# Fetching the down weights of an expert stage from ScalarE's queue, gate and up from SyncE's

## What is computed

```python
def expert_block(args):
    xb, e = args                                   # 128 token rows, an expert
    hid = jax.nn.silu(xb @ w_eg[e]) * (xb @ w_eu[e])    # gate and up, 1024 x 256
    return hid @ w_ed[e]                           # down, 256 x 1024

ys = lax.map(expert_block, (xs, blk_e)).reshape(p_rows, d)
out = jnp.zeros((n, d), h.dtype).at[buf_tok].add(ys * buf_w[:, None])
```

## Time and profile before

| | |
|---|---|
| time, median of 3 runs | 1252.3 us (1246.91 to 1253.53) |
| profiled execution, its own time | 1250.46 us |
| its span, first to last instruction | 1248.4 us |
| TensorE matmul busy | 1108.9 us, 89% |
| VectorE, ScalarE busy | 712.3 us (57%), 564.8 us (45%) |
| hardware DMA queue | 166.65 MB, 38.4% of 16 engines' span |
| software DMA queue | 16.80 MB, 3.6% |

### The profile page before, as it was taken

How to read it: one execution, slowest core, us unless ns; L and a number is a source line. 1 busy time by engine, 2 the same in 40 slices (tenths; PEclk the granted TensorE clock), 3 DMA queues, 4 the chain that set the end, 5 groups by cost and what they waited for, 6 DMA issues and landing times.

```text
span 1248.4 us, 18136 instructions
## 1 busy us (share of the span) xinstructions
PE 1108.9 (89%) x6835; PEld 963.9 (77%) x6835; DVE 712.3 (57%) x832; ACT 564.8 (45%) x756; POOL 327.0 (26%) x276
## 2 busy tenths in 40 slices
PE   3998999999999899999998999329999999999940
PEld 3885888888877788888887888329999999999930
DVE  5874666666055711111114232558888888888838
ACT  5334655655144200000003221407888888888823
POOL 3103222212332223333220000122444444444210
PEclk9988999999999999999999999659999999999975
DMA  7010000021204111111113322537999999999737
GB/s 244 1 28 11 7 7 7 7 69 34 52 1 111 34 34 51 49 37 50 51 51 104 105 75 77 212 121 300 394 368 356 341 348 356 363 379 358 284 141 288
DMA packets 93131, 184.27 MB, mean 148 GB/s; under 512 B 29712, under 2 KB 67088, under 8 KB 79248
## 3 DMA queue, kind: packets, MB, share of 16 engines
q1 hardware_dynamic: 82704, 166.65, 38.4%
q0 software_dynamic: 10368, 16.80, 3.6%
HBM read 177.12 MB, written 27.26 MB: 164 GB/s over the span
## 4 chain that ended last, share of the span: by engine, by line
PE 78%; DVE 11%; ACT 4%; issue 2%; DMA 2%; SPq 1%; POOL 0%; ACTq 0%; POOLq 0%; DVEq 0%
PE ps L369 24%; PE ps L371 23%; PE ps L370 23%; PE ps L858 3%; PE ps L658 2%; DVE pt_lo L1319 1%; PE ps L818 1%; DVE negm L1274 1%; SPq L348 1%; DVE q_tmp L1265 1%; ACT prob L987 1%; DVE acc L1600 1%; DVE res L1610 1%; DVE acc L1601 1%; PE ps L667 1%
## 5 line engine op out<-in xcount | busy, mean ns | idle before, releaser
L1554 DVE TENSOR_TENSOR we_lo<-raw_e,we_hi 128x2048 fp32r<-128x2048 f32 x108 | 246.9, 2288 | 48.3 <-ACT we_hi L1096 48.3
L1096 ACT ACTIVATE we_hi<-raw_e 128x2048 fp32r<-128x2048 f32 x108 | 206.1, 1908 | 8.3 <-DMA raw_e<-in_w_exp_gate_dram 3.7
L369 PE MATMUL ps<-ht_hi,w_hi 128*128 128x512 f32 x448 | 176.4, 394 | 0.4 <-DVE ht_lo L1192 0.4
L371 PE MATMUL ps<-ht_hi,w_lo 128*128 128x512 f32 x448 | 174.7, 390 | 0.0
L370 PE MATMUL ps<-ht_lo,w_hi 128*128 128x512 f32 x448 | 174.6, 390 | 0.0
L369 PE MATMUL ps<-we_hi,xst_hi 128*128 128x256 f32 x576 | 169.4, 294 | 0.0
L370 PE MATMUL ps<-we_lo,xst_hi 128*128 128x256 f32 x576 | 163.5, 284 | 0.0
L371 PE MATMUL ps<-we_hi,xst_lo 128*128 128x256 f32 x576 | 163.4, 284 | 0.0
L363 POOL CAST w_hi<-raw 128x1024 fp32r<-128x1024 f32 x36 | 40.7, 1130 | 302.2 <-PE ps L371 270.3
L369 PEld LDWEIGHTS ps<-we_hi,xst_hi 128*128 128x128 f32 x576 | 111.4, 193 | 0.0
L370 PEld LDWEIGHTS ps<-we_lo,xst_hi 128*128 128x128 f32 x576 | 111.1, 193 | 0.0
(11 more groups left out here) (284 smaller groups left out, 2472.8 us busy)
## 6 DMA issues: line engine op xcount, KB each, us to landing
raw_e<-in_w_exp_gate_dram SPq DMA_DIRECT2D x36, 1024.0 KB, 8.6
raw_e<-in_w_exp_up_dram SPq DMA_DIRECT2D x36, 1024.0 KB, 7.9
raw_e<-in_w_exp_down_dram SPq DMA_DIRECT2D x36, 1024.0 KB, 8.7
raw<-in_w_in_dram SPq DMA_DIRECT2D x27, 512.0 KB, 3.8
yin<-y_dram SPq DMA_DIRECT2D x16, 512.0 KB, 6.6
xin<-in_x_dram SPq DMA_DIRECT2D x8, 512.0 KB, 7.2
raw<-in_w_out_dram SPq DMA_DIRECT2D x8, 512.0 KB, 4.1
xre<-in_x_dram SPq DMA_DIRECT2D x8, 512.0 KB, 4.2
```

What stands on the lines that cost most here:

```text
L369: pe.matmul(dst, st[0], mv[0], start=first, stop=False)
L371: return pe.matmul(dst, st[1], mv[0], start=False, stop=last)
L1096: act.activation(we_hi[c % 4][:, :], raw_e[c % 6][:, :], ACT.Copy).then_inc(sem("w_hi_ready"), 1)
L1554: dve.tensor_tensor(we_lo[c % 4][:, :], raw_e[c % 6][:, :], we_hi[c % 4][:, :].bitcast(F32), ALU.subtract).then_inc(sem("w_lo_ready"), 1)
```

## The change

The function that issues a weight load moves out of SyncE's part and takes the engine as an argument. SyncE keeps the loads of up and gate, and all loads before the first expert. The load of down for expert j+1 is now issued by ScalarE, as the first thing of expert j, ahead of `hidden_high`. Its wait has the same count as before, and in the loop ScalarE reads the expert's number into a register for it.

```diff
+        def load(eng, g, it, j, last=False):
+
+            c, n = piece(g, it, j, last)
+            if isinstance(it, int):
+                src = j
+            else:
+                src = eng.value_load(blk_e[0:1, bass.ds(it * 4 + j, 1)], min_val=0, max_val=NE - 1)
+            wait(eng, "w_lo_ready", n - 5)
+            w_d = (wg_d, wu_d, wd_d)[g]
+            eng.dma_start(raw_e[c % 6][:, :], w_d[bass.ds(src, 1)].rearrange("e p n -> (e p) n")).then_inc(
+                sem(f"raw_e_full{c % 6}"), 16)
...
                 def expert(it, j, left):
                     if left(2):
-                        load(1, it, j + 2)
-                    if left(1):
-                        load(2, it, j + 1, not left(2))
+                        load(sp, 1, it, j + 2)
                     if left(3):
-                        load(0, it, j + 3)
+                        load(sp, 0, it, j + 3)
...
-                load(1, 0, 1)
-                load(2, 0, 0)
-                load(0, 0, 2)
+                load(sp, 1, 0, 1)
+                load(sp, 2, 0, 0)
+                load(sp, 0, 0, 2)
...
                 def expert(it, j, left):
+                    if left(1):
+                        load(act, 2, it, j + 1, not left(2))
                     hidden_high(it, j)
                     if left(2):
                         high(1, it, j + 2)
```

More of the change, by code:

```diff
@@ L494, in _ @@
                 sp.wait_ge(sem("logit_ready"), NT)
[L496 to L505, removed]
                 def expert(it, j, left):
                     if left(2):
-                        load(1, it, j + 2)
-                    if left(1):
-                        load(2, it, j + 1, not left(2))
+                        load(sp, 1, it, j + 2)
                     if left(3):
-                        load(0, it, j + 3)
-                load(0, 0, 0)
-                load(1, 0, 0)
-                load(0, 0, 1)
+                        load(sp, 0, it, j + 3)
+                load(sp, 0, 0, 0)
+                load(sp, 1, 0, 0)
+                load(sp, 0, 0, 1)
                 sp.wait_ge(sem("logit_read"), 1)
-                load(1, 0, 1)
-                load(2, 0, 0)
-                load(0, 0, 2)
+                load(sp, 1, 0, 1)
+                load(sp, 2, 0, 0)
+                load(sp, 0, 0, 2)
                 end = experts(sp, expert)
```

## The result

The changed kernel takes 1286.03 us (median of 4 runs, 1280.06 to 1291.82) against 1249.78 us: ratio 1.0287, 95% interval 1.0255 to 1.0319, 36 us slower. The forecast was slower by 12.7 us, with a range up to 1304. The sign and the place were right, the size was out by nearly three.

A forecast was written before the change was run, and what follows sets the result against it. TensorE was taken to bound the expert stage at 9.94 us an expert. 1250.46 + 12.5 for later down loads + about 0.5 gave 1263.5 for the profiled execution, 1265 us for the median; range 1249 to 1304.

The forecast's parts named there:

- What bounds the kernel: Expert stage: TensorE sets the pace at 9.94 us an expert; no load is waited for, DMA engines nearly full.
- SyncE gains nothing, ScalarE's issue and wait cost nothing: Head of each expert: one load fewer gains SyncE nothing; ScalarE's register read, wait and issue cost 0 directly.
- i = 1.75 us: Time from the start of ScalarE's y copy to the issue of the down load; range 0.8 to 5.0 us.
- case (b): Rival: ScalarE issues only after `xst_hi`, i = 4.3, 1326 us, or 1283 with i = 3.0; chance with (c) 0.23.
- The formula: Expert stage: an expert lasts the longer of 9.94 us and i + L + 1.87 us.
- L = 6.7 us: Down load's time from issue to landing, taken from an up load; expert 10.32 us, 12.5 us lost over 33.
- The regulation of L by itself: Longer experts leave DMA engines more spare time, 0.18 us at 9.94 and 0.54 at 10.3, so a backlog drains.
- The clock: TensorE idling 0.4 to 2 us per expert might lower its clock; given no share up to 10.5 us an expert.
- Case (c): Rival: the DMA backlog stays, L = 7.9, 11.5 us an expert, + 52 us, 1304 us; chance with (b) 0.23.
- Its halfway value: Partly remaining DMA backlog: L = 7.3, 10.9 us an expert, 1284 us.
- the shared 7.9: Upper limit of L in us, by engines taking turns between queues: the down load does not stand behind SyncE's backlog.
- Rival (d), faster,: SyncE's shorter queue lands gate and up loads sooner, helping at best the stage's entry; 1245 us, chance 0.05.

The follow-up runs named there:

- spread rows: A block's tokens laid over the partitions in steps of four instead of from partition 0 up: kernel before 1251.75 us (1.0022), changed kernel 1269.23 us (1.0149).
- the undisturbed kernel above: Changed kernel with ScalarE issuing each down load one expert further ahead (j+2), the second down load on SyncE: 1252.23 us, ratio 1.0016.
- extra copies: Kernel before, ScalarE copying down weights once, twice or three times more into an unused buffer in 8 experts: 1257.63, 1283.32, 1305.55 us.
- steps of 16: Changed kernel with a block's tokens laid over the partitions in steps of 16 (0, 16, 32 ...): 1297.3 us, ratio 1.0395.

## Why the prediction was right or wrong

**What bounds the kernel: right.** With spread rows every load of the kernel before lands sooner and its time stays; a delay of ScalarE by 2.1 us in eight experts costs 5 us, near the 7 that the slack of 1.17 us leaves. Two readings behind it were loose and did no harm. The three VectorE times add up to 3.92 us from 911.08, which is 0.17 too much, as they overlap; 914.83 is right. And the two loads issued at 799.41 and 799.90 did have others about: four more loads of the queue, issued from 795.57 on, were ahead of them. Their landings lie 2.49 us apart all the same.

**SyncE gains nothing, ScalarE's issue and wait cost nothing: right.** The kernel that issues ahead from ScalarE's queue measures 1.0016.

**i = 1.75 us: right in the main.** It is 1.71 in the undisturbed kernel above, 1.54 on average in the nineteen experts that a load held up. The late issue, case (b), did not occur: the issue goes out while the gate split runs. The range, 0.8 to 5.0, missed the other side. After a late load the y copy itself starts late and the next issue does not: at 1027.26 it stands 0.31 us ahead of the y copy, and in all five slowed experts 0.3 to 0.7 us ahead. So the load after a late one is waited for less, 0.6 to 1.6 us in these five.

**The formula: right.** i + L + 1.82 (I had put 1.87) gives the lengths of eighteen of the nineteen experts bound by the load within 0.02 us, and that of the nineteenth, 9.88 us and so hardly held up, within 0.14. For the load issued at 1015.23 it is 1.57 + 10.52 + 1.82 = 13.91, and the two y copies start at 1013.66 and 1027.57.

**L = 6.7 us: this step failed**, and it is the larger part. The nearest row, one up load of the kernel before at 6.7, was a lucky one: the median of the up loads in the same 250 us was 7.9, on record in the same trace. The awaited down loads took 7.56 in the median, 7.96 on average where they set the pace, and 10.5 at most. Two faults lie behind it. I bounded L by bytes and engine shares, from 6.0 to 8.5, as if 16 engines were one; but a load lands with the last of its 16 increments, 7.6 us in the median where the eighth is in by 5.5, and the row traffic sets these apart: without it they stand at 4.9 and 4.7. In the earlier trace rows the rows were only a mean, 1.18 us an expert on each engine. And I put one value into a maximum. The expert lasts the longer of 9.94 and i + L + 1.87, so short landings give nothing back and long ones count in full. Nineteen experts that lost 26.3 us stand beside nine that gained 0.5.

**The regulation of L by itself: half right.** Engines were 89% busy instead of 98%, and the down loads' last increment came at 7.6 instead of 9.1 us. But an expert is lengthened after the late landing, and with rows a late one comes again: 4.0 to 4.9 us of waiting in four experts.

**The clock: wrong.** I gave it no share on the strength of a stretch that is 95% busy. That row says nothing of an idle time in one piece. This is the second step that failed: a term put at nothing. The stage had five idle times of 2.00 to 4.05 us with a fall of the clock, and these five experts cost 10.4 us.

Together: 26.3 + 10.4 - 0.5 = 36.2 us, where the sum had 12.5. Case (c), 11.5 us an expert by a backlog, came near the time (11.05) by another way: the share of the engines fell as foreseen, and L stayed long because of the last increments. Its halfway value, L = 7.3 and 1284 us, lies 2 us from the measured time, but by luck: it has no share for the clock. 10.5 us for one load exceeds the shared 7.9 at which I had seen L end by the rule on turns in the Trainium skill ("DMA: Bandwidth & Descriptors", "Queues, rings and completion order"). The packets of ScalarE's queue in single microseconds, 1019, 1023 and 1024 us, in the changed kernel for that load (packets, MB, share of 16 engines):

```profile
q10 hardware_dynamic: 42, 0.34, 85.8%
...
q1 hardware_dynamic: 34, 0.18, 58.6%
q0 software_dynamic: 84, 0.05, 16.0%
q10 hardware_dynamic: 1, 0.01, 1.9%
...
q1 hardware_dynamic: 25, 0.18, 50.1%
q0 software_dynamic: 43, 0.07, 19.3%
q10 hardware_dynamic: 2, 0.02, 3.9%
```

By 1021 nearly all of the load was in; its last packets trickled until 1025, five in the microsecond from 1021 and then one or two. The engines together were full in 1021 and 1022, but only some three quarters busy in 1023 and 1024. What held these last packets is open.

**Rival (d), faster,** had nothing behind it in any run. No version tried beats the kernel before: its bound is TensorE, and the best of those that do all the work, issuing ahead from ScalarE's queue or spreading the rows, equal it within 0.4%.

## What to carry to other kernels

Moving a load to another engine's queue was free or costly here by one thing, the time between its issue and its use; count the pipeline steps that the new place gives up before anything else, and what the issue then stands behind. Where that time is near the landing time, take the landing's upper end and its spread, not its median: a pipeline pays for late loads and is not repaid by early ones. And do not price a long idle time of TensorE at its length alone: here five of the eight idle times of 1.5 to 4.05 us in the changed kernel, and fifteen of the sixteen of 2.95 to 4.9 us made by extra copies, had a slow stretch behind them that cost 1.4 to 2.6 us more.

## What the runs showed of the hardware

- A 1 MB load lands with the last of its 16 increments, and row traffic of the software queue sets that apart from the rest: the 8th was in by 5.5 to 5.7 us and the last by 7.6 to 9.1 (changed kernel, kernel before), by 4.7 and 4.9 with no row traffic.
- The partitions on which the rows of an indirect DMA lie change its landing and that of the loads beside it. With the same bytes a gather took 8.6 us in the median from partition 0 on and 6.5 in steps of four in the kernel before; in the changed kernel 9.2, 7.4 and, in steps of 16, 10.2.
- A DMA issue on ScalarE goes out while an earlier instruction of ScalarE still runs, and ahead of one that has not begun: the issue at 907.73 stands inside the gate split from 906.94 to 908.84, before `xst_hi` at 908.75.
- After TensorE had idled, the granted clock fell to its lower level for some microseconds and the matmuls of a down product started 0.43 us apart instead of 0.23: after 2.00, 3.19, 3.42, 3.50 and 4.05 us in the changed kernel, after seven of eight idle times of 3.0 us and all eight of 4.9 us in the kernels with extra copies. After 1.54, 1.68 and 2.30 us in the changed kernel it stayed at 1.00.
